# A mixture-of-experts step with its gate and up products cut into four column groups, its activations turned by VectorE, and one token product for two experts

## The chip, the cores and the metric

The kernel runs on one core of a Trainium2 chip. The metric is the device time of one execution in microseconds (us), lower is better. Everything is computed in fp32.

## The reference, cut to what matters

One decoder layer on 320 tokens (256 of a prompt, 64 of samples) of width 1024. The first part (convolutions, cross-attention, gates) is hardly touched by the change. The second is a mixture of experts, 4 of 32 for each token:

```python
def _moe(h, w_router, b_router, w_gu, b_gu, w_dn, b_dn):
    logits = jnp.dot(h, w_router) + b_router
    top_v, top_e = lax.top_k(logits, TOP_K)          # 4 of 32
    gate = jax.nn.softmax(top_v, axis=-1)
    ...
    def expert_block(args):
        xe, e = args
        gu = xe @ w_gu[e] + b_gu[e]                  # 1024 x 2048
        gt, up = jnp.split(gu, 2, axis=-1)
        gt = jnp.minimum(gt, SWIGLU_LIMIT)
        up = jnp.clip(up, -SWIGLU_LIMIT, SWIGLU_LIMIT)
        act = gt * jax.nn.sigmoid(SWIGLU_ALPHA * gt) * (up + 1.0)
        return act @ w_dn[e] + b_dn[e]               # 1024 x 1024
    ...
    y = jax.ops.segment_sum(out * slot_w[:, None], slot_tok, num_segments=t + 1)
```

The result is added to x and normalized. The weights of an expert are 12 MB in fp32, and those of all 32 are read whichever tokens are routed to them.

## The kernel before, in words

The program is written out by hand, one instruction stream for each engine, joined by semaphores; its order is the order of the code.

**Weights.** SP loads the experts' weights in 192 chunks of 2 MB, in the order of STREAM: for each expert four chunks of gate and up rows (c = 0 to 3, two of the eight contraction tiles each), then two chunks of the down weights of the expert before (c = 4, 5). They go round eight places (six in `ring`, two in `ring_low`, which lies in `arena`); the chunk (0, 3) has a place of its own. A chunk is issued (L397, L398) when the chunk that held its place is used up: c = 0 and 1 after their own products (`chunk_used`), c = 2 and 3 after all of gate and up (`gu_done`), c = 4 and 5 after the down products (`dn_done`).

**Tokens.** An expert has up to WIN = 128 slots, in two blocks of BLK = 64. VectorE turns the gathered rows (`turn_tokens`, L1177), so that `xT` holds an expert's slots by columns. The second block is multiplied only for experts with more than 64 tokens, behind a jump (`second_block`, L1684). A count above 128 would need another window; that code (`over_window`) stands in the program behind `If(most > WIN)` and does not run with these inputs.

**One expert on PE** (`window`). `gate_up` (L1704) makes, for each of the eight contraction tiles, the products of one block: `xT` (128 x 64) is the stationary operand, 512 columns of weights move, and the two halves h of the columns go to the two halves of the PSUM partitions, so that two matmuls run side by side. After c = 0 PE turns the activations of the expert before (`turn_act`, eight transposes, L1273), which ACT then copies to `actT` (L786). After c = 1 and c = 2 stand the token products of the expert two before (`to_tokens`, L1776): the outputs `Zs`, 64 slots on each half of the partitions, are multiplied with the gate weights `W` into sums for three tiles of tokens, the tiles 0 and 1 after c = 1 and the tile 2 after c = 2. Then follows `down` of the expert before (L1747), again with two column groups.

**The other engines.** VectorE adds the biases to the sums in PSUM (L1194, L1195), turns the next expert's rows, clips and multiplies (L1199 to L1210; L1210 writes in a strided order), spreads the next biases (L1180), builds the gate weights (`gate_weights`, L1168, L1171) and adds the token sums to x (`add_tokens`, L1149, L1152). ACT takes the sigmoid (L782), moves the down sums to `Zs` (`move_out`, L774) and the turned activations to `actT`.

**Before and behind the experts.** The first expert's rows are gathered on PE by a product with a one-hot matrix (`first_tokens`, L1600), whose stationary operand is every eighth column of the normalized rows XN. `turn_places` (L1631 to L1639) turns the table of slots and `turn_second` (L1273) the second expert's rows, both after `gate_up` of expert 0. Behind the last expert come its token products (`last_tokens`), the final sums (`add_products`), the norm and the stores.

## Time and profile before

| | us |
|---|---|
| median of 3 runs | 1407.25 (1407.15 to 1408.19) |
| the profiled execution | 1407.02 |
| its span, first to last instruction | 1404.9 |
| PE busy | 1340.6 (95%) |
| VectorE busy | 667.7 (48%) |
| ACT busy | 202.9 (14%) |
| chain that ended last: PE / DMA | 83% / 15% of the span |
| HBM, mean over the span | 339 GB/s |

PE is busy to nine tenths or more in all but a few of 40 slices, and in many of the same slices the DMA queues move some 425 GB/s, the most that any slice shows. So a share of busy time doesn't say here which of the two sets the pace; that has to be read stage by stage. The experts run from about 386 us of the span to its end.

### The profile page before, as it was taken

The numbers are of one execution on the slowest core, as the hardware profiler recorded it, in microseconds if no ns is written. First come the engines' busy times: TensorE is split into PE (matmuls) and PEld (weight loads), VectorE is DVE, ScalarE is ACT, GpSimd is POOL, SyncE is SP. The second block draws the span as 40 slices with busy tenths as digits, with TensorE's granted clock in tenths as the row PEclk, the third lists the DMA queues.
The fourth block names the chain that finished last, engine by engine and source line by source line (L and its number), as shares of the span: only waits on it lengthen the run. The fifth ranks groups of instructions, "written<-read, shape, count | busy, mean of one in ns | idle before, by whom it ended". The sixth has DMA issues, their size and how long they took to land.

```text
span 1404.9 us, 15012 instructions
## 1 busy us (share of the span) xinstructions
PE 1340.6 (95%) x6056; PEld 581.3 (41%) x6056; DVE 667.7 (48%) x1058; ACT 202.9 (14%) x303; POOL 177.2 (13%) x177
## 2 busy tenths in 40 slices
PE   7999999999999999999999999999999988888884
PEld 5756766665743333333333333333333322232221
DVE  2997323211534745344434444444475655454552
ACT  4102423201120110000000000000011011100012
POOL 2110100000021211111111111111121121111000
PEclk9999999999799999999999999999999999999997
DMA  9617419356569999979987997998999999999992
GB/s 332 245 51 211 136 60 242 139 220 262 224 252 405 425 422 425 424 316 427 423 337 285 370 409 320 424 424 330 427 425 421 424 423 424 422 426 423 425 427 78
DMA packets 91061, 466.60 MB, mean 332 GB/s; under 512 B 41936, under 2 KB 44268, under 8 KB 66247
## 3 DMA queue, kind: packets, MB, share of 16 engines
q1 hardware_dynamic: 83345, 456.74, 80.5%
q0 software_dynamic: 6240, 5.37, 1.2%
q10 hardware_dynamic: 1374, 3.02, 0.6%
q8 instruction: 77, 1.26, 0.4%
q14 instruction: 25, 0.20, 0.0%
HBM read 472.32 MB, written 4.26 MB: 339 GB/s over the span
## 4 chain that ended last, share of the span: by engine, by line
PE 83%; DMA 15%; issue 1%; DVE 0%; ACT 0%; SPq 0%; DVEq 0%
PE PS L1704 32%; PE PS L1747 15%; PE PS L1333 15%; DMA ring<-in_w_gu 7%; PE PS L1776 7%; DMA ring<-in_w_dn 5%; PE PS L1513 4%; PE PS L1273 3%; DMA arena<-in_w_dn 3%; PE PS L1557 2%; PE PS L1369 2%; PE PS L1600 1%; PE PS L1577 0%; PE PS L1460 0%; DMA XX<-in_x_prompt 0%
## 5 line engine op out<-in xcount | busy, mean ns | idle before, releaser
L1704 PE MATMUL PS<-ring,arena 128*64 128x512 f32 x1824 | 415.2, 601 | 13.2 <-DMA ring<-in_w_gu 11.4
L518 POOL DMA_INDIRECT arena<-h_rows,arena x120 | 153.6, 1280 | 730.8 <-DVE arena L1177 667.1
L1704 PEld LDWEIGHTS PS<-ring,arena 128*64 128x64 f32 x1824 | 125.1, 138 | 277.5 <-issue 275.2
L1333 PE MATMUL PS<-arena,ring 128*128 128x320 f32 x768 | 213.5, 434 | 0.1
L1747 PE MATMUL PS<-ring,arena 128*64 128x512 f32 x880 | 195.6, 594 | 15.6 <-DMA ring<-in_w_dn 15.6
L1149 DVE TENSOR_TENSOR XX<-PS,XX 128x1024 f32<-128x1024 f32 x62 | 73.7, 1221 | 271.7 <-PE PS L1776 271.7
L1333 PEld LDWEIGHTS PS<-arena,ring 128*128 128x128 f32 x768 | 144.2, 190 | 58.7 <-issue 2.0
L1704 PE MATMUL PS<-arena 128*64 128x512 f32 x608 | 137.6, 597 | 3.2 <-DMA arena<-in_w_gu 3.0
L782 ACT ACTIVATE arena<-arena 128x1024 f32<-128x1024 f32 x32 | 33.9, 1058 | 623.2 <-DVE arena L1199 623.2
L1747 PEld LDWEIGHTS PS<-ring,arena 128*64 128x64 f32 x880 | 63.5, 137 | 143.8 <-issue 143.8
L1194 DVE TENSOR_TENSOR arena<-PS,XX 128x1024 f32<-128x1024 f32 x32 | 39.2, 1224 | 122.4 <-PE PS L1704 122.4
L1152 DVE TENSOR_TENSOR XX<-PS,XX 64x512 f32<-64x512 f32 x62 | 42.6, 687 | 101.0 <-PE PS L1776 100.6
L1747 PE MATMUL PS<-arena 128*64 128x512 f32 x336 | 75.6, 594 | 5.9 <-DMA arena<-in_w_dn 5.9
L906 DVE SCALAR_TENSOR_TENSOR arena<-arena,CW 128x256 f32<-128x256 f32 (+1 forms) x256 | 79.6, 387 | 0.0
L1704 PEld LDWEIGHTS PS<-arena 128*64 128x64 f32 x608 | 41.4, 137 | 90.3 <-issue 90.2
L1776 PE MATMUL PS<-arena,XX 64*128 64x512 f32 (+1 forms) x240 | 61.9, 634 | 8.5 <-issue 8.5
L1210 DVE TENSOR_TENSOR arena<-arena 128x1024 f32<-128x1024 f32 x32 | 66.8, 2088 | 3.1 <-ACT arena L782 2.0
L1177 DVE STREAM_TRANSPOSE arena<-arena 128x1024 f32<-128x1024 f32 x30 | 61.1, 2037 | 0.0
L1776 PE MATMUL PS<-arena,W 64*128 64x512 f32 (+1 forms) x216 | 54.1, 612 | 1.6 <-ACT arena L786 1.6
L786 ACT ACTIVATE arena<-PS 128x1024 f32<-128x1024 f32 x32 | 32.8, 1024 | 144.1 <-PE PS L1273 140.7
L1273 PEld LDWEIGHTS PS<-ident,arena 128*128 128x128 f32 (+4 forms) x340 | 37.5, 144 | 29.7 <-issue 26.9
L774 ACT ACTIVATE arena<-PS 128x1024 f32<-128x1024 f32 x32 | 32.8, 1026 | 104.9 <-PE PS L1747 104.9
(207 smaller groups left out, 861.3 us busy)
## 6 DMA issues: line engine op xcount, KB each, us to landing
ring<-in_w_gu SPq DMA_DIRECT2D x96, 2048.0 KB, 19.2
ring<-in_w_dn SPq DMA_DIRECT2D x47, 2048.0 KB, 19.3
arena<-in_w_gu SPq DMA_DIRECT2D x31, 2048.0 KB, 18.6
arena<-in_w_dn SPq DMA_DIRECT2D x17, 2048.0 KB, 21.2
ring<-in_w_in SPq DMA_DIRECT2D x11, 2048.0 KB, 10.9
ring<-in_w_mem_kv SPq DMA_DIRECT2D x2, 2048.0 KB, 20.8
ring<-in_cache_mem_k SPq DMA_DIRECT2D x32, 128.0 KB, 3.3
ring<-in_cache_mem_v SPq DMA_DIRECT2D x4, 1024.0 KB, 6.3
```

The costliest lines, as they stand in the source:

```text
L518: nc.gpsimd.indirect_dma_start(out=XG[e % 2][:, 256 * s:256 * (s + 1)], out_offset=None, in_=h_quarters, in_offset=bass.IndirectOffsetOnAx ...
L906: ins = nc.vector.scalar_tensor_tensor(dst, src, wt, dst, ALU.mult, ALU.add)
L1149: return nc.vector.tensor_tensor(x, PS[:, bank:bank + 2, :], x, ALU.add)
L1152: ins = nc.vector.tensor_tensor(x, token_sum(tt, h, last), x, ALU.add)
L1177: nc.vector.transpose(xT[:].rearrange("p k (s l) -> p s k l", s=Q), XG[e % 2].rearrange("p (s q k) -> p s k q", s=Q, k=KT)).then_inc(main[ ...
L1210: nc.vector.tensor_tensor(gbuf[:].rearrange("p b (j q) -> p b j q", j=4), *grouped, ALU.mult) \
L1273: return nc.tensor.transpose(out, in_, ident[0:n, 0:n])
L1333: last = mm(PS[:, j % 2, 0:T], w[:, k, m * P:(m + 1) * P], hT[:, k, :], start=k == 0, stop=k == KT - 1)
L1513: last = mm(PS[:, 2 + g % 2, 0:T], w[:, k, m * P:(m + 1) * P], ACTS[b][:, k, :], start=k == 0, stop=k == 3)
L1704: last = mm(PS[64 * h:64 * h + 64, 2 * g + b, :], xT[:, k, BLK * b:BLK * (b + 1)], (spare[kk] if m == BONUS else moe_ring(m, 2)[:, kk]) [: ...
L1747: last = mm(PS[64 * h:64 * h + 64, 4 + b, :], actT[:, b, j, c * BLK:(c + 1) * BLK], moe_ring(AT[(e, 4 + c)], 4)[:, j, h * 512:(h + 1) * 51 ...
L1776: ins = mm(token_sum(tt, h, last), W[e % 2][64 * h:64 * h + 64, b, tt * P:tt * P + ROWS[tt]], Zs[64 * h:64 * h + 64, b, :], start=start, s ...
```

## The change

**Gate and up.** For each contraction tile the 64 slots of a block are taken as two parts of 32 (i), and for each part the columns in four groups q: 256 gate columns and the 256 up columns that belong to them move together as 512. The group q writes the PSUM partitions 32q to 32q + 31. One block of one chunk is 16 matmuls with a stationary operand of 128 x 32, before it was 8 with 128 x 64.

**Activations.** The sums now stand as 32 slots by 256 columns in each quarter of the partitions, so VectorE's 32 x 32 transposes turn them (`turn_act`, two instructions), straight to `actT`. PE's transposes and ACT's copy are gone. The down weights are loaded as (p j) rows, four of a partition's eight with each chunk, and the biases in quarters, to fit.

**Token products.** `Zs` holds the outputs of two experts, the even one on partitions 0 to 63 and the odd one on 64 to 127, over all 1024 columns. ACT moves each expert's sums there in two pieces, one of them across the halves. A product now contracts over 128 partitions, and there is one for two experts, after c = 1 and c = 2 of the odd experts from 3 on. Whether the second block is taken is decided by the larger count of the pair. For the last expert VectorE makes the crossing copy (`cross_last`).

**The jump.** `If(most > WIN)` now stands ahead of the last two experts, whose code is in both of its branches, on PE, ACT and VectorE.

**The start.** ACT copies each tile of XN into an order in which the stationary operands of `first_tokens` lie together (`regroup`); `turn_places` moves from expert 0 to c = 1 of expert 2; `gate_up` waits for both bias sums at its first matmul.

```diff
-            nc.vector.tensor_scalar(GD[0:r, tt], EX[0:r, tt, None, :].to_broadcast([r, Q, NE]), gden[0:r, tt:tt + 1],
...
+        def regroup(tt):
+            r = ROWS[tt]
+            act.wait_ge(ffn_normed, tt + 1)
+            if tt == 2:
+                act.wait_ge(first_used, 1)
+            nc.scalar.activation(grouped[tt % 2][0:r], XN[0:r, tt, :].rearrange("p (q k) -> p k q", k=KT), ACT.Copy) \
+                .then_inc(regrouped, 1)
+            keep_rows(tt)
...
-            nc.scalar.activation(Zs[:], PS[:, 4:6, :], ACT.Copy).then_inc(main["zs_ready"], 1)
...
+            if n > 1 and e % 2 == 0:
+                act.wait_ge(main["tok_done"], TT * (n // 2))
+            straight = nc.scalar.activation(Zs[own, :, 512 * (e % 2):512 * (e % 2) + 512], PS[own, 4:6, :], ACT.Copy)
+            if e < NE - 1:
+                straight = nc.scalar.activation(Zs[own, :, 512 * (1 - e % 2):512 * (2 - e % 2)], PS[other, 4:6, :], ACT.Copy)
+            straight.then_inc(main["zs_ready"], 1)
...
-                act.wait_ge(main["ta_done"], NE * v + e + 1)
-                nc.scalar.activation(actT[:].rearrange("p b j t -> p b (j t)"), PS[:, 6:8, :], ACT.Copy) \
-                    .then_inc(main["actT_ready"], 1)
...
+        def turn_act(v, e):
+            n = NE * v + e + 1
+            dve.wait_ge(main["act_ready"], n)
+            if n > 1:
+                dve.wait_ge(main["dn_done"], n - 1)
+            for b in range(2):
+                rows = gbuf[:, b:4:2, :].rearrange("p i (q j) -> p i j q", j=KT)
+                last = nc.vector.transpose(actT[:, :, BLK * b:BLK * (b + 1)].rearrange("p j (i l) -> p i j l", i=2), rows)
+            last.then_inc(main["actT_ready"], 1)
...
+        def cross_last(v):
+            dve.wait_ge(main["dn_done"], NE * (v + 1))
+            nc.vector.tensor_copy(Zs[BLK:P, :, 0:512], PS[0:BLK, 4:6, :]).then_inc(main["zs_crossed"], 1)
...
-                    for h in range(2):
-                        last = mm(PS[64 * h:64 * h + 64, 2 * g + b, :], xT[:, k, BLK * b:BLK * (b + 1)],
-                                  (spare[kk] if m == BONUS else moe_ring(m, 2)[:, kk])
-                                  [:, g * D + h * 512:g * D + (h + 1) * 512],
-                                  start=k == 0, stop=k == KT - 1)
+                    w = (spare[kk] if m == BONUS else moe_ring(m, 2)[:, kk]).rearrange("p (g q n) -> p g q n", g=2, q=4)
+                    for i in range(2):
+                        at = BLK * b + 32 * i
+                        for q in range(4):
+                            last = mm(PS[32 * q:32 * q + 32, 2 * i + b, :].rearrange("p (g n) -> p g n", g=2),
+                                      xT[:, k, at:at + 32], w[:, :, q, :], start=k == 0, stop=k == KT - 1)
...
-                ins = mm(token_sum(tt, h, last), W[e % 2][64 * h:64 * h + 64, b, tt * P:tt * P + ROWS[tt]],
-                         Zs[64 * h:64 * h + 64, b, :], start=start, stop=stop)
+                ins = mm(token_sum(tt, h, last), W[:, b, tt * P:tt * P + ROWS[tt]], Zs[:, b, 512 * h:512 * (h + 1)],
+                         start=start, stop=stop)
...
+                    if n == 2 and c == 1:
+                        turn_places()
+                    if e >= 3 and e % 2 and c in (1, 2):
...
-        window(0)
+        window(0, 0, LATE)
+
         with pe.If(most > WIN):
+            window(0, LATE, NE)
             over_window(1)
...
+            last_tokens(1, bd_done)
             pe.nop()
-        last_tokens(0, bd_done)
+        with pe.Else():
+            window(0, LATE, NE)
+            last_tokens(0, bd_done)
+            pe.nop()
```

How this moves instructions. First PE within an odd expert, from its chunk c = 1 to its chunk c = 2 (`gate_up` is L1704 and then L1752, the token products L1776 and then L1812; x is the number of matmuls; what stands behind a COMPARE_AND_BRANCH up to the next UNCONDITIONAL_BRANCH is the second block, jumped over in most experts). Before:

```order
L1273 MATMUL PS<-ident,arena 128x128 [waits tok_added,act_ready]
L1273 MATMUL PS<-ident,arena 128x128 x7
L1684 COMPARE_AND_BRANCH [waits loaded5]
L1704 MATMUL PS<-ring,arena 64x512 x8
L1684 UNCONDITIONAL_BRANCH
L1704 MATMUL PS<-ring,arena 64x512 x8
L1797 COMPARE_AND_BRANCH [waits w_ready,zs_ready,actT_ready]
L1776 MATMUL PS<-arena,XX 128x512 x8
L1797 UNCONDITIONAL_BRANCH
L1776 MATMUL PS<-arena,XX 128x512 x4
```

Now:

```order
L1729 COMPARE_AND_BRANCH [waits loaded5]
L1752 MATMUL PS<-ring,arena 32x512 x16
L1729 UNCONDITIONAL_BRANCH
L1752 MATMUL PS<-ring,arena 32x512 x16
L1829 TENSOR_LOAD arena [waits w_ready,zs_ready]
L1829 ISA x2
L1830 COMPARE_AND_BRANCH
L1812 MATMUL PS<-arena,W 128x512 x8
L1830 UNCONDITIONAL_BRANCH
L1812 MATMUL PS<-arena,W 128x512 x4
```

The transposes are gone, a gate/up chunk has twice the matmuls, the token products are as many as before but stand in every second expert only, and the pair's count is loaded right ahead of their jump.

Second PE at the end. Before: expert 31's down products, the jump over `over_window` (L1880), and, behind all of that code, expert 31's token products:

```order
L1747 MATMUL PS<-arena 64x512 [waits low_in1,zs_ready,actT_ready]
...
L1747 MATMUL PS<-ring,arena 64x512 x8
L1880 COMPARE_AND_BRANCH [waits w_ready,zs_ready]
...
L1880 UNCONDITIONAL_BRANCH
L1689 TENSOR_LOAD arena
L1689 ISA x2
L1797 COMPARE_AND_BRANCH
L1776 MATMUL PS<-arena,XX 128x512 x8
```

Now, first the jump, between expert 28's down products and expert 30's loads of counts, then the end of the branch that is taken:

```order
L1783 MATMUL PS<-ring,arena 64x512 x8
L1912 COMPARE_AND_BRANCH
L1734 TENSOR_LOAD arena
L1734 ISA x2
...
L1783 MATMUL PS<-ring,arena 64x512 x8
L1829 TENSOR_LOAD arena [waits zs_ready,zs_crossed,w_ready,tok_added]
L1829 ISA x2
L1830 COMPARE_AND_BRANCH
L1812 MATMUL PS<-arena,W 128x512 x8
L1812 MATMUL PS<-arena,W 64x512 x4
```

Between the last down products and the last token products there is now no code that is not run but the second block's.

Third VectorE in an odd expert, from the product of the activations on. Before:

```order
L1210 TENSOR_TENSOR arena<-arena 128x1024 [waits sig_done,prod]
L1180 STREAM_SHUFFLE XX<-arena 128x1024
L1168 STREAM_SHUFFLE RGs<-XX 128x640 [waits w_ready]
L1171 SCALAR_TENSOR_TENSOR W<-RGs,slotpos 128x320 [waits rows_spread]
L1171 SCALAR_TENSOR_TENSOR W<-RGs,slotpos 128x320
```

Now:

```order
L1248 TENSOR_TENSOR arena<-arena 128x1024 [waits sig_done,prod]
L1212 STREAM_SHUFFLE XX<-bias 128x512
L1189 STREAM_SHUFFLE XX<-XX 128x640 [waits tok_done,w_ready]
L1192 SCALAR_TENSOR_TENSOR W<-XX,slotpos 128x320 [waits rows_spread]
L1192 SCALAR_TENSOR_TENSOR W<-XX,slotpos 128x320
L1208 STREAM_TRANSPOSE arena<-arena 128x2x8x32 [waits dn_done,act_ready]
L1208 STREAM_TRANSPOSE arena<-arena 128x2x8x32
```

The transposes come last, behind the gate weights, and wait for the down products of the expert before.

## Rows read from the trace of the kernel before

**Rows 1.** Stages: length; busy PE, PEld, DVE, ACT, POOL; clock, DMA share, GB/s
```profile
512.00:960.00 448.00, 448.00 (x2084) 150.96 (x2082) 196.41 (x216) 39.23 (x38) 65.66 (x51) 1.00 0.91 378
960.00:1120.00 160.00, 159.06 (x740) 53.23 (x738) 94.12 (x103) 18.66 (x18) 31.08 (x24) 1.00 1.00 421
1130.00:1376.00 246.00, 211.14 (x952) 69.71 (x954) 123.75 (x140) 25.84 (x25) 25.78 (x21) 1.00 1.00 419
```

**Rows 2.** Timeline of PE, one small expert: start, us, line, forms, count
```profile
465.19 1.09 PE L1273 MATMUL PS<-ident,arena 128*128 128x128 f32 x8
466.21 3.65 PE L1704 MATMUL PS<-ring,arena 128*64 128x512 f32 x16
469.79 1.99 PE L1776 MATMUL PS<-arena,XX 64*128 64x512 f32 x8
471.71 3.65 PE L1704 MATMUL PS<-ring,arena 128*64 128x512 f32 x16
475.30 1.08 PE L1776 MATMUL PS<-arena,XX 64*64 64x512 f32 x4
```

**Rows 3.** Timeline of PE, token products of a large expert; gate/up of the next
```profile
597.26 3.71 PE L1776 MATMUL PS<-arena,XX 64*128 64x512 f32 x16
...
604.48 1.94 PE L1776 MATMUL PS<-arena,XX 64*64 64x512 f32 x8
606.34 10.52 PE L1704 MATMUL PS<-ring,arena 128*64 128x512 f32 x48
616.69 3.60 PE L1747 MATMUL PS<-ring,arena 128*64 128x512 f32 x16
```

**Rows 4.** Timeline of PE, a chunk in the last third of the experts
```profile
1130.08 3.65 PE L1704 MATMUL PS<-arena 128*64 128x512 f32 x16 [1.32 <-DMA arena<-in_w_gu]
```

**Rows 5.** Groups of PE by line and form: four column groups (128*32), full width (128*128)
```profile
L1369 PE MATMUL PS<-ring,arena 128*128 128x512 f32 x64 | 27.6, 592 | 0.0
...
L1460 PE MATMUL PS<-XX,arena 128*32 128x256 f32 x64 | 5.1, 391 | 0.0
L1479 PE MATMUL PS<-ring,arena 128*32 128x128 f32 x128 | 5.0, 273 | 0.0
```

**Rows 6.** Groups of PE by line, 365 to 388 us
```profile
L1600 PE MATMUL PS<-arena,XX 128*128 128x128 f32 (+1 forms) x48 | 12.9, 450 | 0.0
```

**Rows 7.** Stretches with the granted clock (third number from the end), columns as in rows 1
```profile
369.40:389.90 20.50, 20.50 (x86) 16.67 (x87) 9.46 (x38) 3.22 (x6) 0.00 (x0) 0.50 0.63 259
...
1386.60:1396.80 10.20, 5.68 (x12) 1.47 (x12) 3.49 (x4) 2.48 (x5) 0.00 (x0) 0.50 0.02 3
```

**Rows 8.** Timeline of PE, from the end of expert 0's gate/up to expert 1's
```profile
405.65 1.07 PE L1631 MATMUL PS<-ident,arena 128*128 128x128 f32 x6
...
407.98 1.16 PE L1273 MATMUL PS<-ident,arena 128*128 128x128 f32 x8
410.21 5.35 PE L1704 MATMUL PS<-ring,arena 128*64 128x512 f32 x16 [1.06 <-ACT arena L760]
```

**Rows 9.** Timeline of PE, the last experts' down and token products
```profile
1365.85 3.65 PE L1747 MATMUL PS<-arena 128*64 128x512 f32 x16 [1.40 <-DMA arena<-in_w_dn]
...
1375.10 3.65 PE L1747 MATMUL PS<-arena 128*64 128x512 f32 x16
```

**Rows 10.** The chain that ended last, its end: start, us, what
```profile
1382.24 1.03 ACT arena L774
1383.27 7.41 issue
1390.67 3.81 PE PS L1776 x8
```

**Rows 11.** Groups of VectorE by line, 421 to 1376 us
```profile
L1149 DVE TENSOR_TENSOR XX<-PS,XX 128x1024 f32<-128x1024 f32 x60 | 71.2, 1220 | 249.3 <-PE PS L1776 249.3
...
L1177 DVE STREAM_TRANSPOSE arena<-arena 128x1024 f32<-128x1024 f32 x30 | 61.1, 2037 | 0.0
```

**Rows 12.** DMA queues of the page: packets, MB, share
```profile
q8 instruction: 77, 1.26, 0.4%
```

274 lines of the change are left out of this document (139 added, 135 removed).

## The prediction

> **What bounds the kernel now.** I read the table of stages first, since the page's shares of busy time can't separate PE from the DMA queues. It shows three stages of the experts [rows 1]. From 512 to 960 us PE has no idle time and the queues move 378 GB/s at a share of 0.91: PE sets the pace, and the queues run dry now and then because it gives back places too late. From 960 to 1120 us both are full. From 1130 to 1376 us the queues are at 1.00 and PE is idle for 35 of 246 us: there the weights set the pace, a chunk of 2.1 MB at 419 GB/s in 5.0 us, and PE awaits it from the queue and needs about 3.6 us for it [rows 4]. So a gain on PE counts in full up to the last point where the queues run dry. That is expert 17: in the timeline of PE six experts have a second block (5, 7, 10, 11, 14 and 17; the last gate/up run of such an expert is x48 in one piece, as in rows 3), and after 960 us the share stays at 1.00. What PE gains behind that turns into waiting. Last comes the tail behind the last chunk: the chain of waits has 7.41 us there in which PE waits for nothing that the profile shows, between ACT's last copy and expert 31's token products [rows 10].
>
> A small expert costs PE 3.58 us for a gate/up chunk (466.21 to 469.79), 1.02 for the transposes (465.19 to 466.21) and 1.92 and 1.01 for the token products [rows 2]; a large one's token products take 3.64 and 1.87, less than 0.1 of overlap taken off [rows 3].
>
> **The change, part by part.**
>
> *Gate and up in four groups.* The columns streamed stay the same: twice the matmuls, four side by side in place of two. Uncut, 48 records (two for a matmul) take 10.35 us, that is 24 rounds of two groups at 0.431 us [rows 3], which is also what one full-width record of 512 columns takes (27.6 us by 64, [rows 5]). What a round of four costs at 512 columns no row shows. Nearest are the attention's products in four groups, eight bursts of each kind [rows 5]: 8 records of 256 columns in 0.64 us, of which the last record is 0.39, so 0.25 for one round; 16 records of 128 columns in 0.625 us less 0.27, so 0.118 for each of three rounds. Scaled to 512 columns that is 0.50 and 0.47, both with the start of a short burst in them; the lower bound is 0.431. I take 0.434, near the lower end: full-width products show no more than the columns once a run is long, and the longer burst is the lower of the two. Up to the end of expert 17's gate/up there are 17 experts and 5 second blocks (6 with its own), 22 to 23 blocks of 32 rounds, some 704 rounds: +2 us; the bounds are 0 and +27.
> The Trainium skill speaks against the choice: "TensorE: Matmul & The Clock Gate", section "Measured speedup vs the span model", has three column groups at 2.38 times one and four row groups at 3.07, not 3 and 4. That is a rival below.
>
> *Transposes off PE.* 17 x 1.02: **-17.3 us**. On VectorE they are two instructions of half the size of L1177, which takes 2.04 us [rows 11], so about 2.0 together. They hide: VectorE is busy for 196 of 448 us [rows 1], and the down products come a whole gate/up (14 us) and the other expert's down behind the sums. In return token sums and gate weights come once for two experts.
>
> *Token products.* A product for two experts contracts over 128 partitions, but its two halves no longer run side by side. At 0.431 us a record, a small pair is 12 records: 5.2 us and two seams of 0.2, 5.6 in place of 2 x 2.93. If either expert is large, both blocks are taken: 10.8, in place of 2.93 + 5.51 where one is, 11.0 where both are. Up to expert 17's sums the pairs (0,1) to (14,15) are due: four small, three mixed, one with both. Before 11 x 2.93 + 5 x 5.51 = 59.8; now 4 x 5.6 + 4 x 10.8 = 65.6. **+5.8 us**, a loss.
>
> *Seams.* Four gate/up chunks with three cuts take about 14.2 us, four uncut ones 4 x 3.45 = 13.8 [rows 2, 3]. Even experts have no cut now, the eight odd ones two: 17 x 0.4 less 8 x 0.27 is **-4.6 us**.
>
> *The start.* `first_tokens` is 48 records in 12.9 us, 0.27 each for 128 columns [rows 6], where four-group records of 128 columns need under 0.12 a round: the strided stationary operand sets that pace. But most of it lies where the clock is granted at 0.5 (1.2 GHz) [rows 7]; at half of 2.4 GHz the 128 columns alone take twice their 0.11, so there only 0.05 a record is to be had. With the clock as it was, 16 records gain 2.3 us and 32 gain 0.05 each, -4; if denser work keeps it up, to -9. I take -4.5. Behind expert 0's gate/up PE needs 4.56 us to expert 1's first matmul (405.65 to 410.21, [rows 8]): `turn_places`, `turn_second`, a copy. Now `turn_second` (1.16) and a copy run beside VectorE's two bias sums, for which that matmul newly waits, two of 1.22 [rows 11]; with latency 2.6 us. **-2.0.** `turn_places` (405.65 to 407.98) comes back in expert 2, **+2.3**. The regrouping copies lie on ACT beside PE's work; only the third could be seen, 1 us.
>
> Sum at expert 17: 2 - 17.3 + 5.8 - 4.6 - 6.5 + 2.3 = **-18 us**. The queues are full from there with the same bytes, so the last chunk lands 18 us earlier.
>
> *The tail.* The chunk (30, 5) is awaited until 1365.85; two more at 5.0 us each land the last at about 1375.7. Before, the last down products start at 1375.10, kept back by transposes, copy and token products, and end at 1382.2 [rows 9, 10]. Now none of these stands before them, their first half is done by the landing if VectorE's transposes end 3.5 us ahead of it (by the durations above they end just so), and the second half ends 3.6 us behind it, not 6.6. **-3.0.** VectorE's crossing copy (about 1.2) beside ACT's 1.03: +0.2. The 7.41 us are a jump over two windows of code that isn't run; queue 8 brings code in pieces of 16 KB (1.26 MB in 77 packets, [rows 12]), and these must come first. Now the jump stands ahead of expert 30, and the way to the last products is a load and a short branch: an estimate of 1.2 us between 0.6 and 3, **-6.2**. Eight records took 3.81 us at clock 0.5 [rows 7, 10]; eight full ones at 1.0 take 3.6, as PE idles only some 2.5 us before: -0.2. Sum **-9 us**.
>
> The moved jump is paid by PE before expert 30. There PE has about 1.4 us over on each chunk, and ten chunks follow before the tail: 14 us, less 2.6 for the pair's longer products in expert 31. Without that cover it costs up to 7 us.
>
> Together -18 - 9 = -27 on the profiled execution's 1407.0: **1380.0 us**. The median of the runs shown is 0.2 above it, which changes nothing.
>
> **The rivals.**
> (a) *Four groups don't run at full*, the one that ends slower. Each ns more a round costs 0.70 us up to expert 17. The gain of 29 us (27 and the 2 above) is used up at 0.431 + 0.041 = 0.472 us a round; at 0.50 the kernel takes 1407 - 29 + 49 = 1427. For it: no run of four groups of more than four rounds is seen, and four streams of weights are read at once while the queues write. Against: 0.47 has a burst's start in it [rows 5]. Chance 0.10.
> By the skill's 2.38 of 3 the round would be 0.54 us and the time about 1457; rows 5 leave little room for that.
> (b) *Code supply.* Gate/up doubles PE's instructions. If the 7.41 us stand for two pieces of code at 3.7, PE stalls where it passes a piece faster than that, which the jumps over second blocks could bring about. 1 us in each of 17 experts: 1397. For it: the jump's price. Against: no idle time at the 26 jumps of before. Chance 0.08.
> The Trainium skill, "Runtime: NRT & Kernel Launch", section "Instruction fetch mechanics", has code fetched in sequence in 16 KB blocks, and a wait for a jump out of the window; by that the far jump costs in its new place what it did, and the short ones nothing.
> (c) *Little gain in the middle*: a round of 0.445 and the large pairs leave -9 there; with the tail 1389 to 1397. Chance 0.17.
> (d) *The moved jump isn't covered*, or the clock drops in the tail (full products at 0.5 take 3.5 us more): 1384 to 1389. Chance 0.10.
> The forecast, 1371 to 1384, has 0.55.
>
> **How the numbers follow.** 0.2% is 2.8 us, about what a measurement of this kernel can tell from no change. Only (a) reaches break-even: slower 0.09, within 0.2% 0.03, faster 0.88. The range goes from 1371 (start at -9, rounds at 0.431, a short tail) to 1398, through (b) and (c); (a) and the outermost of the others lie outside.
>
> **What would show it.** Gate/up of a small even expert in one run of 13.8 us; more than 14.5 means (a). No transposes of PE beside the experts. Token groups of 3.6 and 1.9 us in odd experts only. A DMA share above 0.91 from 512 to 960 us, the last chunk 18 us earlier, expert 1 near 404. A gap of PE of 5 to 9 us before expert 30, and about 1 us in place of the 7.41. The prediction is wrong if the middle isn't shorter by 10 us, or if a wait for `actT_ready` or `zs_ready` stands in PE's list.

## The result, and the profile after

The change takes 1369.3 us (median of 4 runs, 1368.9 to 1371.5) beside 1407.2 before (median of 4, 1404.7 to 1408.2): a ratio of 0.9736, with a 95% interval of 0.9720 to 0.9753. Measured again with the last experiments it took 1371.65 us (5 runs, 1369.5 to 1373.9; ratio 0.9756, 0.9741 to 0.9772). The forecast was 1380, from 1371 to 1398: faster it is, by 35 to 38 us and not by 27, and the first measurement lies below the range. The profiled execution of the change took 1369.1 us with a span of 1367.0, against 1407.0 and 1404.9, and its rows are what is compared here. Times on the span below are those of each kernel's own profile.

Some words used below. A matmul has two records in the profile. A **round** is one record on each of the column groups that work side by side. A **switch** is the place where PE goes from one kind of product to another (gate and up, `down`, token products). A **place** is one of the eight buffers of 2 MB that the weights' chunks go round in.

The table of stretches of the kernel after [rows 1, 7]:

```profile
core 0: us, PE busy (x) PEld busy (x) DVE busy (x) ACT busy (x) POOL busy (x), PEclk, DMA share, GB/s
369.40:389.90 20.50, 19.61 (x176) 12.31 (x179) 13.01 (x67) 5.28 (x7) 1.12 (x1) 1.00 0.94 371
512.00:960.00 448.00, 448.00 (x3186) 137.81 (x3180) 184.55 (x207) 41.31 (x40) 60.61 (x56) 1.00 0.95 396
960.00:1120.00 160.00, 142.47 (x991) 42.84 (x988) 75.25 (x84) 17.52 (x17) 21.64 (x20) 1.00 1.01 423
1130.00:1340.00 210.00, 173.10 (x1156) 50.36 (x1148) 92.43 (x105) 20.09 (x20) 17.25 (x16) 0.97 1.00 421
```

From 512 to 960 us PE is still without idle time, and the queues move 396 GB/s in place of 378. From 960 us on PE is idle for 18 of 160 us where it had 1: the weights now set the pace already there. The first row is the surprise: the clock stays at 1.00 where it was 0.50. It does so in 12 of the 16 profiled kernels that have this start; in the other four the mean of the same stretch is 0.75 to 0.83.

PE's timeline after, the start (L1645 is `first_tokens`, L1752 gate and up, L1318 `turn_second`); it answers to rows 6 and 8:

```profile
367.14 2.05 PE L1645 MATMUL PS<-arena 128*128 128x128 f32 x16
371.64 1.16 PE L1645 MATMUL PS<-arena 128*128 128x128 f32 x8
374.74 3.14 PE L1645 MATMUL PS<-arena 128*128 128x128 f32 x24
377.95 3.64 PE L1752 MATMUL PS<-ring,arena 128*32 128x512 f32 x32
395.49 1.16 PE L1318 MATMUL PS<-ident,arena 128*128 128x128 f32 x8
398.20 3.94 PE L1752 MATMUL PS<-ring,arena 128*32 128x512 f32 x32 [1.55 <-DVE arena L1234]
```

The 48 records of `first_tokens` take 6.35 us, not 12.9, and expert 1's first matmul starts at 398.20, not at 410.21. The middle of the same timeline (L1783 is `down`, L1812 the token products), which answers to rows 2 and 3; first an odd expert with a small pair, then an even one, then an odd one with a large pair:

```profile
451.67 3.70 PE L1812 MATMUL PS<-arena,W 128*128 128x512 f32 x8
455.30 3.64 PE L1752 MATMUL PS<-ring,arena 128*32 128x512 f32 x32
...
459.87 1.08 PE L1812 MATMUL PS<-arena,W 128*64 128x512 f32 x4
460.88 3.64 PE L1752 MATMUL PS<-ring,arena 128*32 128x512 f32 x32
...
471.47 3.64 PE L1752 MATMUL PS<-arena 128*32 128x512 f32 x32
474.93 10.48 PE L1752 MATMUL PS<-ring,arena 128*32 128x512 f32 x96
485.34 7.09 PE L1783 MATMUL PS<-ring,arena 128*64 128x512 f32 x32
...
507.06 3.70 PE L1812 MATMUL PS<-arena,W 128*128 128x512 f32 x8
510.69 3.64 PE L1752 MATMUL PS<-arena 128*32 128x512 f32 x32
514.26 1.08 PE L1812 MATMUL PS<-arena,W 128*64 128x512 f32 x4
515.27 3.64 PE L1752 MATMUL PS<-arena 128*32 128x512 f32 x32
```

Gate and up of the even expert take 485.34 - 471.47 = 13.87 us for 32 rounds. The transposes are gone. The token products of a small pair take 3.63 and 1.01 us from start to start. (Both odd experts here show a pair with one block; a pair with two takes 7.06 and 1.87.) Last, the moved jump and the tail, in PE's timeline and in the chain of waits [rows 9, 10]:

```profile
1274.34 3.65 PE L1783 MATMUL PS<-ring,arena 128*64 128x512 f32 x16 [0.61 <-DMA ring<-in_w_dn]
1284.01 1.03 PE L1752 MATMUL PS<-ring,arena 128*32 128x512 f32 x1 [6.01 <-issue]
1288.12 12.66 PE L1752 MATMUL PS<-ring,arena 128*32 128x512 f32 x92 [3.08 <-issue]
...
1341.99 3.65 PE L1783 MATMUL PS<-arena 128*64 128x512 f32 x16 [2.50 <-DVE arena L1208]
1346.90 3.65 PE L1783 MATMUL PS<-ring,arena 128*64 128x512 f32 x16 [1.25 <-DMA ring<-in_w_dn]
```

```profile
1350.60 1.23 DVE arena L1216
1351.83 1.05 issue
1352.87 3.71 PE PS L1812 x8
```

The jump costs 6.01 and 3.08 us ahead of expert 30, and in the tail 1.05 us stand where 7.41 stood. From the landing of the last chunk (1346.6) to the end are 20.4 us, 29.5 before. The page's part on DMA queues has more pieces of code than before [rows 12]:

```profile
q8 instruction: 102, 1.67, 0.5%
```

**A row that no view prints.** A chunk comes in 16 parts, and PE waits for the last of them. From the trace's records of the chunk's semaphore I took when the first and the last part landed, in us of the span, for chunk (18, 3), behind which the queues of the changed kernel run dry for the last time, and for the last chunk, (31, 5). The spread is the time from the first to the last part of (31, 5). The pieces of code are those of queue 8, in the whole execution and between the two landings:

```
                               (18,3) first  last    (31,5) first   last  spread   pieces: all, between
before                              953.4   955.2        1368.8  1375.4     6.6       77    28
after                               920.5   922.3        1335.4  1346.6    11.2      102    41
after, once more                    923.6   925.5        1338.7  1349.1    10.5      102    41
jump behind all experts             921.4   923.4        1336.3  1344.4     8.0      102    38
two groups from expert 20 on        925.1   927.0        1340.0  1346.6     6.6       90    29
two groups everywhere               918.0   919.8        1331.4  1338.3     6.9       70    27
token products beside down          919.7   921.6        1328.7  1337.8     9.1      102    41
the same, once more                 920.5   922.5        1329.6  1339.3     9.7      102    41
down in four groups as well         920.3   923.5        1334.1  1344.0     9.9      118    48
one-element matmuls added           924.2   926.0        1391.2  1392.7     1.5      114    49
```

The first part of the last chunk is 33.3 us earlier than before the change, the last part only 28.8. At chunk (18, 3) both are 32.9 earlier; the difference grows where the queues are full.

### The profile page after: what moved, and what is told of

Its sections match the earlier page's. It is cut to its first block, busy times and chain, and to the rows that moved or that the text cites. A ratio compares the mean times of both kernels' runs of the same rounds, so it can differ in the third digit from the quotient of the medians.

```text
span 1367.0 us, 18938 instructions
## 1 busy us (share of the span) xinstructions
PE 1283.7 (94%) x8028; PEld 532.4 (39%) x8028; DVE 606.4 (44%) x1013; ACT 207.6 (15%) x305; POOL 153.6 (11%) x177
## 4 chain that ended last, share of the span: by engine, by line
PE 78%; DMA 20%; DVE 1%; issue 1%; ACT 0%; SPq 0%; DVEq 0%
PE PS L1752 30%; PE PS L1378 15%; PE PS L1783 15%; DMA ring<-in_w_gu 12%; DMA ring<-in_w_dn 7%; PE PS L1812 6%; PE PS L1558 4%; PE PS L1602 3%; PE PS L1414 2%; PE PS L1318 1%; PE PS L1645 0%; PE PS L1505 0%; DMA XX<-in_x_prompt 0%; PE PS L1524 0%; PE PS L1622 0%
## 5 line engine op out<-in xcount | busy, mean ns | idle before, releaser
L1752 PE MATMUL PS<-ring,arena 128*32 128x512 f32 x3648 | 411.5, 599 | 37.8 <-DMA ring<-in_w_gu 27.1
L1752 PEld LDWEIGHTS PS<-ring,arena 128*32 128x32 f32 x3648 | 117.4, 110 | 322.5 <-issue 313.8
L1783 PE MATMUL PS<-ring,arena 128*64 128x512 f32 x880 | 196.5, 595 | 10.8 <-DMA ring<-in_w_dn 10.8
L1752 PE MATMUL PS<-arena 128*32 128x512 f32 x1216 | 137.8, 594 | 9.1 <-DMA arena<-in_w_gu 9.0
L1783 PEld LDWEIGHTS PS<-ring,arena 128*64 128x64 f32 x880 | 60.9, 137 | 144.5 <-issue 144.5
L1812 PE MATMUL PS<-arena,W 128*128 128x512 f32 (+1 forms) x252 | 97.9, 605 | 2.3 <-issue 2.3
L1208 DVE STREAM_TRANSPOSE arena<-arena 128x512 f32<-128x512 f32 x64 | 68.1, 1105 | 31.6 <-PE PS L1783 31.6
L1783 PE MATMUL PS<-arena 128*64 128x512 f32 x336 | 75.5, 595 | 5.4 <-DMA arena<-in_w_dn 2.9
L1752 PEld LDWEIGHTS PS<-arena 128*32 128x32 f32 x1216 | 40.0, 110 | 101.8 <-issue 101.8
L1812 PEld LDWEIGHTS PS<-arena,W 128*128 128x128 f32 (+1 forms) x252 | 35.2, 171 | 64.4 <-issue 64.4
L1783 PEld LDWEIGHTS PS<-arena 128*64 128x64 f32 x336 | 23.8, 137 | 56.0 <-issue 56.0
L1244 DVE SCALAR_TENSOR_TENSOR arena<-arena 128x1024 f32<-128x1024 f32 x32 | 39.2, 1226 | 3.6
## 6 DMA issues: line engine op xcount, KB each, us to landing
ring<-in_w_dn SPq DMA_DIRECT2D x47, 2048.0 KB, 20.1
```

The lines of the kernel that those rows point to most:

```text
L1208: last = nc.vector.transpose(actT[:, :, BLK * b:BLK * (b + 1)].rearrange("p j (i l) -> p i j l", i=2), rows)
L1752: last = mm(PS[32 * q:32 * q + 32, 2 * i + b, :].rearrange("p (g n) -> p g n", g=2), xT[:, k, at:at + 32], w[:, :, q, :], start=k == 0, st ...
L1783: last = mm(PS[64 * h:64 * h + 64, 4 + b, :], actT[:, 4 * c + j, b * BLK:(b + 1) * BLK], moe_ring(AT[(e, 4 + c)], 4)[:, j, h * 512:(h + 1) ...
L1812: ins = mm(token_sum(tt, h, last), W[:, b, tt * P:tt * P + ROWS[tt]], Zs[:, b, 512 * h:512 * (h + 1)], start=start, stop=stop)
```

## The experiments

All start from the changed kernel. Its own time differs by up to 4 us from one measurement to the next (1369.3, 1371.9, 1373.3 and 1371.65), and the start of expert 0 by 2.4 us; so times are compared with a repeat of the changed kernel that was measured beside them, or by rows. The first four had no such repeat: their differences from 1369.3 carry those 4 us, and what they show is read from rows.

**1. The jump behind all experts again**, on every engine (PE shown):

```diff
-        window(0, 0, LATE)
+        window(0, 0, NE)
         with pe.If(most > WIN):
-            window(0, LATE, NE)
             over_window(1)
...
         with pe.Else():
-            window(0, LATE, NE)
             last_tokens(0, bd_done)
```

> The changed kernel with the jump over the large-count windows put back behind all 32 experts, on every engine; all else as changed. Theory: in its old place the jump costs PE its full price between the last ACT copy and the last token products (1.05 us of it now, 7.4 before), and the two stalls of PE before expert 30 (6.0 and 3.1 us) vanish without moving the last chunk, since PE has time over there: +6.2 us, some 1375.5. Rival: the stall before expert 30 is what costs the queues 4 to 5 us of their lead between experts 24 and 31 (the last chunk lands 28.7 us earlier than before the change, the chunks up to (24, 0) 33.2 earlier); then the last chunk now lands 3 to 5 us earlier still and the sum is +1 to +3, some 1371. Second rival: the jump costs less in this kernel than 7.4 in its old place, since its windows of code are laid out otherwise: +3 or less with no move of the last chunk.

Measured: 1375.66 us (1375.2 to 1377.9), span 1373.2: +6.2 on the span, the number of the theory. But its parts are others. PE's timeline, and a row of the chain of waits:

```profile
1281.21 3.64 PE L1752 MATMUL PS<-ring,arena 128*32 128x512 f32 x32 [2.68 <-DMA ring<-in_w_gu]
...
1341.21 5.35 PE L1783 MATMUL PS<-arena 128*64 128x512 f32 x16 [2.63 <-DVE arena L1208]
1346.36 3.63 PE L1783 MATMUL PS<-ring,arena 128*64 128x512 f32 x16
1356.24 7.64 PE L1812 MATMUL PS<-arena,W 128*128 128x512 f32 x12 [6.24 <-issue]
```

```profile
1351.26 4.97 issue
```

The stall before expert 30 is gone, and the last part of the last chunk lands 2.2 us earlier (1344.4), which the first rival foresaw. Little of that arrives: PE begins the second half of the last down products, which waits for that chunk, at 1346.36 and not at 1344.4, since its first half is held back by VectorE (2.63) and runs at a lower clock (5.35 us where the changed kernel has 3.65). So this second half starts 0.5 us earlier than in the changed kernel (1346.90). From its start to the end are 26.8 us in place of 20.1: the jump 3.9 more (4.97 in the chain, where 1.05 stood), and the token products 2.9 more (7.64 in place of 4.71; the granted clock is 0.76 in the mean from 1350 us to the end). So the moved jump gains 6.7 us behind the last chunk, nearly half of that by the clock, and its new place costs 0.5 of it. The second rival was right that the jump costs less here in its old place than before the change (4.97, not 7.41); that the total still came out at +6.2 is luck.

**2. Two column groups for gate and up.** The sums land on other partitions and the activations come out permuted, so this kernel serves for its time alone:

```diff
-                        at = BLK * b + 32 * i
-                        for q in range(4):
-                            last = mm(PS[32 * q:32 * q + 32, 2 * i + b, :].rearrange("p (g n) -> p g n", g=2),
-                                      xT[:, k, at:at + 32], w[:, :, q, :], start=k == 0, stop=k == KT - 1)
+                        for q in range(2):
+                            last = mm(PS[64 * q:64 * q + 64, 2 * i + b, :].rearrange("p (g n) -> p g n", g=2),
+                                      xT[:, k, BLK * b:BLK * b + BLK], w[:, :, 2 * i + q, :], start=k == 0, stop=k == KT - 1)
```

> The changed kernel with gate and up multiplied in two column groups of 64 slots instead of four of 32 (half the matmul instructions, same columns streamed; the sums land on other partitions, so the activations are permuted). Theory: a round of four groups (0.434 us) costs what a round of two does (0.431), so the uncut gate and up of an even expert takes 13.8 us in both and the time is 0 to 2 us lower, 1367 to 1369. Rival: doubling PE's instructions costs something beside the rounds (code supply, seams of chunks): 5 us or more lower, below 1364. Rival on the other side: two groups lose their even feed from shared weights, slower by over 2 us.

Measured: 1362.17 us (1358.3 to 1363.2), some 7 us less; the rival was right that something beside the rounds costs. Times from start to start of PE's runs, between 500 and 935 us, each the same to a few ns over its occurrences, show what ("tiles 0, 1" and "tile 2" are token products; the last column is experiment 7):

```
                                      before   after   two groups   down in four (7.)
32 rounds of gate/up, then down            -  13.871       13.733       13.733
24 rounds of gate/up, then down       10.351  10.438       10.300       10.324
16 rounds of gate/up, then tiles 0, 1  7.018   7.005        6.967        6.980
8 rounds of gate/up, then tile 2       3.584   3.571        3.484        3.571
16 rounds of down, then gate/up        6.867   7.017        6.866        6.867
tiles 0, 1 of a small pair, gate/up        -   3.631        3.631        3.631
tile 2 of a small pair, then gate/up       -   1.009        0.859        1.009
```

64 uncut rounds of an expert with a second block take 27.605 us in the changed kernel and 27.467 with two groups: the same 0.138 apart as 32. So a round of four groups costs what one of two does, 0.4292 us, and each switch away from four-group gate and up costs 0.14 us, whatever follows. With two groups it costs nothing in front of `down`, 0.05 in front of tile 2 and 0.10 in front of tiles 0 and 1. The way back costs 0.15 from `down` or tile 2 and nothing with two groups; from tiles 0 and 1 it costs 0.20 in both. With two groups PE is 6.3 us shorter from expert 2 to expert 18. A further 4 us come from the queues: the spread of the last chunk is 6.9 us, not 11.2. Against these stand an expert 2 that starts 2.0 us later, within what repeats differ by, and a tail of 21.9 us in place of 20.4, with the last token products at a lower clock (6.29 us, not 4.71).

**3. The strided operand for `first_tokens`** (the regrouping copies are still made):

```diff
-                last = mm(PS[:, half, (k % 4) * P:(k % 4 + 1) * P], grouped[tt % 2][0:r, k, :], hot[0:r, tt % 2, :],
+                last = mm(PS[:, half, (k % 4) * P:(k % 4 + 1) * P], XN[0:r, tt, k:D:KT], hot[0:r, tt % 2, :],
```

> The changed kernel with first_tokens taking every eighth column of the normalized rows again as stationary operand; the regrouping copies are still made and awaited. Theory: the contiguous operand is what kept the clock at 1.00 from 369 to 414 us of the span. Strided, the 48 records take 12 to 13 us again instead of 6.3, the granted clock falls to 0.5 in and behind them, gate and up of expert 0 take 3 us more, and the kernel is 8 to 10 us slower: about 1378. Rival: the clock was kept up by other things of the change; then only the 48 records are longer, by some 0.11 each, and the kernel is about 5 us slower: 1374. Second rival: the third regrouping copy and not the stride sets the pace there: no difference.

Measured: 1380.59 us (1379.9 to 1381.7), span 1378.9, +11.9. PE's timeline and two stretches:

```profile
369.50 4.19 PE L1645 MATMUL PS<-arena,XX 128*128 128x128 f32 x16
...
377.94 2.27 PE L1645 MATMUL PS<-arena,XX 128*128 128x128 f32 x8
...
382.04 6.40 PE L1645 MATMUL PS<-arena,XX 128*128 128x128 f32 x24
388.37 5.06 PE L1752 MATMUL PS<-ring,arena 128*32 128x512 f32 x32
```

```profile
369.40:389.90 20.50, 20.50 (x94) 17.90 (x97) 10.53 (x43) 4.79 (x7) 0.00 (x0) 0.53 0.72 298
379.40:399.90 20.50, 20.50 (x128) 13.29 (x131) 9.31 (x54) 3.22 (x6) 1.12 (x1) 0.71 0.51 195
```

The 48 records take 12.86 us again, double, and the clock falls again: 0.53 in the stretch in which the changed kernel has 1.00, 0.71 in the one ten us later; with it the first chunk of gate and up of expert 0 takes 5.06 in place of 3.64. Expert 2 starts 11.7 us later than in the changed kernel, and 9.7 to 11.6 later than in experiments 1, 2 and 4. The first theory stands, somewhat larger than expected: the contiguous operand is worth 10 to 12 us.

**4. Eight transposes on PE again**, of a constant, ahead of every `down`:

```diff
+            for b in range(2):
+                for j in range(4):
+                    tr(PS[:, 4 + b, j * P:(j + 1) * P], ident[:, :])
```

> The changed kernel with eight transposes of a constant added on PE before the down products of every expert (what the old turn_act cost PE, 1.02 us for each expert; their results are overwritten, nobody waits for them). Theory: time on PE counts in full up to the point from which the queues are full, expert 17 to 20, and not behind it: the start of expert 17's gate and up is 17 us later, the last chunk 17 to 20 us later, the kernel 17 to 20 us slower: about 1387. Rival: in the middle the changed kernel is already paced by the weights here and there (share 0.95), so only a part counts: +10 or less. Rival on the other side: all 32 count, +32: about 1401.

Measured: 1386.38 us (1383.2 to 1388.9), span 1385.2, +18.2. The start of expert 17 is 16.0 us later (905.2, 889.2), that of expert 18 17.1, the last chunk's last part 15.1 (1361.7), and 3.1 come in the tail, where the transposes stand in PE's way again. So the transposes of the experts behind 18 move the last chunk by nothing. The stretch from 512 to 960 us has the DMA share of before the change again, 0.91:

```profile
512.00:960.00 448.00, 448.00 (x3207) 144.49 (x3209) 178.40 (x199) 40.26 (x39) 56.31 (x52) 1.00 0.91 381
```

This is the main term of the prediction, and the rule under it: PE's time counts nearly in full up to there (16.4 us of transposes from expert 2 to expert 18 make that stretch 15.5 longer), and not behind it.

**5. Tile 2's products one by one**, both halves of the columns on the same partitions:

```diff
...
-            return PS[:, 6 - 2 * tt + half, :] if tt < 2 else PS[64 * half:64 * half + r, 6, :]
+            return PS[:, 6 - 2 * tt + half, :] if tt < 2 else PS[0:r, 6 + half, :]
...
```

> The changed kernel with tile 2's token products (64 tokens) written for both halves of the columns to the same 64 partitions, in two PSUM banks, instead of one half to each half of the partitions. Theory: the two halves ran side by side in the changed kernel; one by one the group of tile 2 takes 1.75 us in place of 1.01 for a small pair and 3.5 in place of 1.87 for a pair with a large expert. Up to expert 17 four pairs of each: 4 x 0.75 + 4 x 1.65 = 9.6, the kernel +8 to +10: about 1378. Rival: they were as short for another reason (only 64 columns of stationary operand): no difference.

Measured: 1382.01 us (1378.8 to 1386.2), 10.1 us more than the repeat of the changed kernel beside it (1371.9). Its timeline has for tile 2 of a small pair

```profile
464.69 1.93 PE L1812 MATMUL PS<-arena,W 128*64 128x512 f32 x4
466.55 3.64 PE L1752 MATMUL PS<-ring,arena 128*32 128x512 f32 x32
```

1.86 us from start to start in place of 1.01, and 3.58 in place of 1.87 for a large one. Four of each are 10.2 us; from expert 2 to expert 18 the kernel is 10.3 longer. In the changed kernel the two halves do run side by side.

**6. Token products beside the down products.** In odd experts gate and up are uncut, tiles 1 and 0 stand ahead of `down`, tile 2 behind it:

```diff
...
+                        some_tokens((1, 0))
+                        pe.wait_ge(main["tok_added"], TT * i + 1)
                     down(v, e - 1, previous)
+                    if e >= 3 and e % 2:
+                        pe.wait_ge(main["tok_added"], TT * i + 2)
+                        some_tokens((2,))
```

> The changed kernel with gate and up of odd experts left uncut: the token products of tiles 1 and 0 go directly before the down products, those of tile 2 directly behind them, and VectorE's adds and gate weights move accordingly. Theory: a switch from gate and up's 32-slot column groups to another kind of product costs 0.14 us and the way back 0.15 (down 7.017 us to the next gate/up in the changed kernel, 6.866 with two groups; gate/up 13.871 against 13.733), at the cuts for token products too. Two of three such round trips of an odd expert go: 0.5 us less in each, up to expert 17 some 4 us, the kernel 3 to 4 us faster: 1365 to 1366. Rival: PE now waits before the down products for VectorE's sum of tile 1, up to 0.6 us each: no gain. Second rival: the gate weights and the activations come too late on VectorE, seen as waits for actT_ready or w_ready: slower.

Measured: 1365.05 us (1363.4 to 1368.6), and once more:

> The kernel with the token products beside the down products, once more, beside the changed kernel on the same chip: 4 to 7 us faster than it (3.5 by the switches of PE that it saves up to expert 17; 6.9 was measured beside an unintended repeat).

1364.75 us (1362.6 to 1365.9). Beside the repeats of the changed kernel (1371.9 and 1371.65) that is 6.9 less, both times. PE's timeline, a large pair:

```profile
588.67 7.13 PE L1813 MATMUL PS<-arena,W 128*128 128x512 f32 x16
595.74 3.65 PE L1784 MATMUL PS<-ring,arena 128*64 128x512 f32 x16
599.22 3.60 PE L1784 MATMUL PS<-arena 128*64 128x512 f32 x16
602.65 1.89 PE L1813 MATMUL PS<-arena,W 128*64 128x512 f32 x8
604.47 3.64 PE L1753 MATMUL PS<-arena 128*32 128x512 f32 x32
```

No wait stands between them. Up to expert 18 PE is only 2.1 us shorter (511.5 us from expert 2 on, 513.6 in the changed kernel), half of what I had expected of the switches: what is saved is the 0.14 in front of each token product within gate and up (304.5 us in all, 306.7 before the edit), while the 0.20 behind tiles 0 and 1 stays (7.06 for 16 records in front of `down` as in front of gate and up). The rest comes at the last hole of the queues, which is expert 17's. There the changed kernel has on PE

```profile
903.08 7.13 PE L1812 MATMUL PS<-arena,W 128*128 128x512 f32 x16
910.15 3.64 PE L1752 MATMUL PS<-arena 128*32 128x512 f32 x32
913.72 1.94 PE L1812 MATMUL PS<-arena,W 128*64 128x512 f32 x8
915.58 3.64 PE L1752 MATMUL PS<-arena 128*32 128x512 f32 x32
919.04 7.05 PE L1752 MATMUL PS<-ring,arena 128*32 128x512 f32 x64
926.02 7.09 PE L1783 MATMUL PS<-ring,arena 128*64 128x512 f32 x32
```

With 9 us of token products inside, gate and up end at 926.0, and only then chunks (17, 4) and (17, 5) are issued (from 926.2 in the trace), while the queues had emptied with chunk (18, 3) at 922.3. Uncut, the two are issued from 915.6 on (916.5 in the repeat), before the queues are empty; the last part of (17, 4) lands at 926.5 in place of 933.5. The first part of the last chunk is 6.7 us earlier than in the changed kernel, the last one 8.8, of which PE makes use of 7.3: the second half of the last down products starts at 1339.6, not at 1346.9. So by the rows what the version saves is a place that is handed back late, more than the switches; no run changes the one without the other.

**7. Down products in four groups as well** (two slot halves by two column halves):

```diff
...
-                    for h in range(2):
-                        last = mm(PS[64 * h:64 * h + 64, 4 + b, :], actT[:, 4 * c + j, b * BLK:(b + 1) * BLK],
+                    for q in range(4):
+                        h, i = divmod(q, 2)
+                        last = mm(PS[32 * q:32 * q + 32, 4 + b, :], actT[:, 4 * c + j, b * BLK + 32 * i:b * BLK + 32 * i + 32],
...
```

> The changed kernel with the down products in four column groups of 32 slots as well (two slot halves by two column halves, the same sums in the same places, twice the down instructions). Theory: the 0.14 and 0.15 us of a switch come from the change of the tile's size; with down at 32 too both vanish between gate/up and down, 0.29 us an expert, 5 us up to expert 17. Against that stand some 0.25 MB more of code, which the DMA engines bring beside the weights; kernel 2 to 4 us faster. Rival: the switch cost is not of the tile's size (it comes from other banks or from a full pipeline of loads): PE as before, and the kernel the same or 2 us slower by the code.

Measured: 1367.57 us (1367.1 to 1367.8), 4.3 less than the repeat beside it. The table in 2. has it: 13.733 and 6.867, the switch costs between gate/up and down are gone behind uncut runs (0.02 is left behind the 24 rounds of a cut one), while those before and behind tile 2 (3.571, 1.009) stay. So the cost between gate/up and `down` belongs to the change of the tile's size from 32 to 64 columns. And with 16 pieces of code more than the changed kernel (7 of them between the two landings) the spread is 9.9 us, no more than in the repeats.

**8 and 9. More code, without work.**

> The changed kernel with 256 instructions that do nothing on ACT in every expert (ACT is idle there; 0.5 MB more of code, what PE's doubled gate and up added). Theory: the code of all engines comes over the same 16 DMA engines as the weights, and unevenly: in the stretch in which the queues are full the last of a chunk's 16 parts falls further behind the first (11.2 us at the last chunk in the changed kernel, 6.6 before the change, 6.9 with two groups), and PE waits for the last part. Then the first part of the last chunk lands as now (within 1 us) and the last one 3 to 5 us later: kernel +3 to +5, about 1373. Rival: the spread has nothing to do with code: no difference in spread or time.

> The changed kernel with 256 instructions that do nothing on PE ahead of the down products of every expert from 20 on, where PE waits for weights anyway: 12 pieces of code of 16 KB more. Theory of the code beside the weights: the spread of the last chunk's 16 parts grows from 11 to about 15 us and the kernel by 3 to 5 us beyond what the instructions cost PE itself. Rival: spread 11, and only PE's own time for them, if it isn't hidden.

Neither tells anything of code: the instructions that do nothing didn't come (18938 instructions in the profile, 102 pieces of code, as in the changed kernel). They are two repeats of it, 1371.9 us (1371.8 to 1372.9) and 1373.3 (1370.1 to 1374.5), with spreads of 10.8 and 10.4 us. They show how far repeats lie apart.

**10. Two groups from expert 20 on**, by the edit of 2. under `if e >= 20` (the activations of these experts are permuted):

> The changed kernel with gate and up in two column groups of 64 from expert 20 on, and in four before (the activations of the experts from 20 on are permuted). From expert 20 the queues are full, so PE's own time counts little there; what changes is that PE's code for 12 experts is smaller by some 12 pieces of 16 KB. Theory: PE's code comes beside the weights and holds up some of the 16 parts of a chunk. Up to expert 20 all is as in the changed kernel; the first part of the last chunk lands within 1 us of now, the spread of its 16 parts falls from 11 to about 7 us, the kernel is 3 to 5 us faster: 1365. Rival: the spread comes from something else (the gathers of tokens, the place of the jump): spread 10 to 11, kernel within 1 us, 1368 to 1370.

Measured: 1366.6 us (1365.4 to 1370.7), 6.7 less than the repeat beside it (1373.3). The first part of the last chunk lands 414.8 us behind that of chunk (18, 3); in the changed kernel it is 415.0, and 415.1 once more. So the queues' pace is the same, and only the parts stay together: the spread is 6.6 us. The last products on PE:

```profile
1346.88 3.65 PE L1788 MATMUL PS<-ring,arena 128*64 128x512 f32 x16
1352.94 6.29 PE L1817 MATMUL PS<-arena,W 128*128 128x512 f32 x12 [2.41 <-issue]
```

So the spread of the parts, some 4 us, goes with PE's doubled gate and up in the last third of the experts. How much of it the kernel gets is less certain. The execution that was profiled is the slowest of its four (1370.7), no faster than the profiled one of the repeat (1370.1): it enters the last third 2.9 us later, which is scatter of the first part, gains 3.9 on PE from there to the second half of the last down products, and loses 1.6 again, since the last token products run at a lower clock (6.29 us, not 4.71).

**11. One-element matmuls** (64 ahead of `down`, from expert 20 on), as code that does little:

> The changed kernel with 64 one-element matmuls on PE ahead of the down products of every expert from 20 on (one row, 64 columns of stationary operand, one column moved; about 3 us of PE in each, where PE waits some 8 us for weights anyway; 16 KB of code each, 11 to 12 pieces more). With 12 pieces less (two groups from expert 20 on) the spread of the last chunk's 16 parts fell from 10 or 11 us to 6.6. Theory: with 12 more it grows to 14 or 15 us, first part as now, the kernel 3 to 5 us slower than the changed kernel of this call. Rival: two groups cut the spread by something else than code (fewer instructions a microsecond on PE, other timing of its semaphores): spread 10 to 11, time within 2 us.

Measured: 1459.65 us (1457.5 to 1460.9). The dose was wrong:

```profile
1068.94 9.44 PE L1794 MATMUL PS<-ones,iota_s 1*64 1x1 f32 x128
1078.30 5.00 PE L1783 MATMUL PS<-arena 128*64 128x512 f32 x16
```

The 64 (two records each) take 9.4 us, 0.15 each; four such products in the changed kernel, before expert 2's third chunk, take 0.33 us from start to start, 0.08 each, and I had reckoned with 0.05. PE became the bound (98% busy), the queues weren't full, and the spread went to 1.5 us with 49 pieces of code between the landings, more than in any other kernel here. It doesn't test what it was made for, but it shows that code alone makes no spread: the queues must be full.

**12 to 14. Versions.** With the jump ahead of expert 24 (`LATE = NE - 8`), on top of 6.:

> The kernel with the token products beside the down products (run before, 1365), with the jump over the large-count windows ahead of expert 24 instead of 30. Theory: PE is stalled 6 to 9 us there, early in the stretch in which the queues are full, and has eight experts to make it up; the last chunk lands 1 to 2 us earlier, as it did with the jump behind all experts (2.4 earlier), and the tail keeps the short branch: 1363 to 1364. Rival: the place of the stall doesn't matter once it is covered: 1365. Rival on the other side: at expert 24 PE has no lead yet, the queues run dry for part of it: 1367 or more.

1364.12 us (1362.6 to 1365.9): within the scatter of 6. With the down products of odd experts in four groups, on top of 6.:

> The kernel with the token products beside the down products (run before, 1365), with the down products of odd experts (those that follow an uncut gate and up directly and lead to the next one) in four column groups as well; those of even experts, which stand between token products, stay in two. Theory: 0.29 us less for each such expert, eight up to expert 17: 2.3 us, less some 0.5 for the code: 1363. Rival: the code of the added instructions takes all of it: 1365 to 1366.

1365.59 us (1362.3 to 1367.6): no gain to be told either. All three, and the changed kernel once more:

> Token products beside the down products, the down products of odd experts in four groups, and the jump ahead of expert 24: the three parts that were tried one by one. Theory: the parts add up, 1 to 3 us faster than the kernel with the first alone. Rival: the code of the added instructions and the earlier stall take it back: within 1 us.

> The changed kernel itself, once more. The two kernels with instructions that do nothing turned out to hold none of them (the same number of instructions and of pieces of code as the changed kernel), so they were repeats of it: 1371.9 and 1373.3 beside the 1369.3 of the first measurement. This one gives the changed kernel's time beside the three others of this call: 1369 to 1373.

1363.14 us (1361.8 to 1364.9; ratio 0.9699, 0.9686 to 0.9712) against 1371.65 (1369.5 to 1373.9). The three together beat the changed kernel by 8.5 us, and the first alone by 6.9; between the two the ranges overlap.

## Why the prediction was right and wrong

**The sum by its own steps.** On PE from expert 2's gate and up to expert 18's (532.5 us before, 513.6 after), and the start before it:

```
                                        forecast   measured
rounds +2, seams -4.6                       -2.6       +0.5   (gate/up and down: 453.6 to 454.1)
transposes off PE (17; 16 in this stretch) -17.3      -16.4
token products                              +5.8       -5.4   (59.7 to 54.3)
turn_places back                            +2.3       +2.3
the start, up to expert 2 (one group
of transposes, 1.0, in it)                  -6.5      -14.3
the sum at expert 17 or 18                 -18        -33.2
last part of the last chunk                -18        -28.8
tail                                        -9         -9.1
```

So the miss of 11 us is what is left of larger ones that partly cancel. The gain was forecast 11.2 us too small on the token products and 6.9 on the start and the transposes, and 3.1 too large on the seams and 4.4 behind expert 18.

**Right:** that PE's time counts up to the point where the queues are full (4.), the transposes, the tail as a whole and in parts (down 6.8 to 4.0 us behind the landing, -2.9, where -3.0 was said; the copy +0.2; the jump -6.4 for -6.2; the products -0.1 for -0.2), and that the rounds run at full. Rival (a) is dead: 0.4292 us a round, in runs of 64 as of 32, which is also what a full-width record takes (8 more records of tiles 0 and 1 are 3.43 us). The Trainium skill, in "TensorE: Matmul & The Clock Gate", section "Measured speedup vs the span model", has three column groups at 2.38 times one; four groups of 32 columns with 512 moved show no such loss here, and here the measurement decides.

**Wrong, first: the step "a product for two experts contracts over 128 partitions, but its two halves no longer run side by side".** It holds for tiles 0 and 1. Tile 2 has 64 tokens, and its two halves still go to different column groups. A small pair costs 4.64 us and not 5.6, a large one 8.93 and not 10.8; 4 x 0.96 + 4 x 1.87 = 11.3 us, all of the difference of that row, and 5. gives 10.2 of it back. The rows read before had it: among the token products those of tile 2 alone have 64 stationary columns (64*64 beside 64*128 in rows 2, 128*64 beside 128*128 now). It was priced as if it had 128.

**Wrong, second: the size of the start.** The mechanism was named, with an end at -9 for a clock that stays up; the working value took the clock as it was. 3. shows that the stride both doubled the time and let the clock fall, and that the two together are worth 10 to 12 us. The change is 8.5 us ahead at expert 0's first matmul (386.47, 377.95), 12.0 at expert 1's and 14.3 at expert 2's. The clock was treated as given where the change itself moved it, if not in every execution.

**Wrong, third: the seams.** The cuts were priced at 0.4 us for the three of an expert and 0.27 for the two of an odd one, from the two-group rows; the switches between gate and up and `down` at nothing; and the four-group rounds at +0.003 each. In truth the rounds cost nothing more. Beside its rounds (704 of 0.4292 are 302.2) gate and up took 309.4 us before and 306.7 now, a gain of 2.7; `down` went from 144.2 to 147.4, of which 2.4 are sixteen switches back at 0.15 and 0.8 a wait for weights. So the new switches take back what the missing cuts gave.

**Not foreseen: the queues gave back 4.5 us.** The sentence "the queues are full from there with the same bytes, so the last chunk lands 18 us earlier" holds for the first of a chunk's 16 parts (-33.3 at the end, -32.9 at chunk (18, 3)), not for the last (-28.8). Of rival (b), code supply, this may be a relative: PE's code didn't stall PE (no idle time from 512 to 960 us), but late in the kernel the parts of a chunk drift apart. Undoing the doubled matmuls there takes 4 us of the spread away (10.), the jump's old place 2.4 to 3.2 (1.). In the table the spread goes with the pieces of code between the landings from 27 to 41 (6.6 to 11.2 us), and no further: with 48 it is 9.9 (7.). So the bytes of the code alone don't explain it, and its cause stays open; the runs that were to add code and nothing else added none (8, 9) or too much work (11).

**Rival (d)**, the moved jump not covered, is in small part right: 9.1 us of stall, of which 2.2 reach the last chunk and 0.5 PE's last down products. The Trainium skill's "Runtime: NRT & Kernel Launch", section "Instruction fetch mechanics", has a jump out of the window wait for its code. The trace agrees that there is a stall wherever the jump stands. That it costs the same in both places, as the prediction read it, the rows don't bear out: 6.01 and 3.08 in the new place, 4.97 in the old one in this kernel, 7.41 before the change.

The range ended at 1371, made from a start at -9, rounds at 0.431 and a short tail. It had no term for a mistake about the token products, which were taken as known. One sign that was to mean a wrong prediction did come: a wait for `actT_ready` stands in PE's list, 2.50 us before expert 31's first down products. It costs nothing in this kernel, since they still end (1345.6) before the last chunk has landed (1346.6). One slip in the chances: "slower" and "within 0.2%" add up to 0.12, but only (a) was to get there, and it had 0.10.

## What to carry to other kernels

Price a merged product by the output shape of each of its tiles: a tile with 64 rows keeps its two column groups even where the others lose them. Keep products of one tile size together, and put what interrupts a long run beside another interruption; the switches are saved, and above all the places that would be handed back late. Where a queue is full, follow the last part of a transfer to the end, not its first. And check a total that comes out as forecast by its parts: in 1. the +6.2 was made of a cheaper jump and a lower clock.
